# Attention value products with stationary values, heads in pairs on the two halves of the output rows

## The reference, cut to what matters

```
logits = einsum('bqhd,bqkhd->bhqk', q, k_sel) * scale - slopes * dist
p = softmax(logits, axis=-1)
return einsum('bhqk,bqkhd->bqhd', p, v_sel)      # per head: probabilities times values
...
o = concatenate([o_a, o_b], axis=-1)
return o @ w_out
```

## Time and profile before

| | |
|---|---|
| median of 3 runs | 2524.43 us (2522.5 to 2528.1) |
| the profiled execution: its own time | 2525.57 us |
| its span (first to last instruction) | 2523.8 us, 35771 instructions |
| PE busy | 2448.3 us, 97% of the span, 13860 matmul records |
| DVE, ACT, POOL busy | 1185.3 us (47%), 951.8 us (38%), 1053.6 us (42%) |
| `mixers` on PE | from about 468 to 940 us of the span |
| products with values, L1314 | 576 records, between 503.3 and 907.9 us |

### The profile page before, as it was taken

One profiled execution on the slowest core, in us unless ns is written; L12 is line 12 of the kernel. 1 busy time (PEld: TensorE's weight loads), 2 busy tenths in 40 slices (PEclk: granted clock), 3 DMA queues, 4 the chain that ended last, 5 costly groups with the idle time before them and its releaser, 6 DMA issues.

```text
span 2523.8 us, 35771 instructions
## 1 busy us (share of the span) xinstructions
PE 2448.3 (97%) x13860; PEld 2107.5 (84%) x13860; DVE 1185.3 (47%) x2304; ACT 951.8 (38%) x1614; POOL 1053.6 (42%) x584
## 2 busy tenths in 40 slices
PE   7999999889999989999999999999999999999996
PEld 7889999768888778899998888888888888888885
DVE  6798985445555433333333365323365432232224
ACT  3687883333443323322223333322333222332222
POOL 0434123365554314443343544444444444355342
PEclk9999999899999999999999999999999999999999
DMA  4101230334333233323332323232333233333431
GB/s 140 35 18 38 99 100 29 104 97 129 105 102 104 81 108 113 113 84 89 96 101 84 92 75 117 84 109 82 93 101 101 75 109 100 100 93 107 117 93 50
DMA packets 275000, 231.40 MB, mean 92 GB/s; under 512 B 10768, under 2 KB 255568, under 8 KB 274832
## 3 DMA queue, kind: packets, MB, share of 16 engines
q1 hardware_dynamic: 266640, 220.59, 29.3%
q10 hardware_dynamic: 8192, 8.52, 1.0%
HBM read 215.81 MB, written 12.71 MB: 91 GB/s over the span
## 4 chain that ended last, share of the span: by engine, by line
PE 60%; DMA 1%; ACT 1%; POOL 1%; DVE 1%; issue 0%; POOLq 0%; SPq 0%; ACTq 0%; DVEq 0%
PE banks L2043 38%; PE banks L2077 19%; PE banks L2109 1%; PE banks L1764 1%; DMA last_draw<-in_w_down 0%; PE banks L2068 0%; PE banks L2071 0%; POOL dL L1986 0%; PE banks L2095 0%; DMA cq_raw<-in_w_up 0%; POOL wL L1979 0%; ACT dH L2161 0%; DVE y L2301 0%; ACT hH L1774 0%; DVE n_bn L1673 0%
## 5 line engine op out<-in xcount | busy, mean ns | idle before, releaser
L1979 POOL TENSOR_TENSOR wL<-cq_raw,wH 128x2048 fp32r<-128x2048 f32 x87 | 407.8, 4687 | 521.5 <-ACT wH L2155 521.5
L2043 PE MATMUL banks<-hL,wH 128*128 128x512 f32 (+1 forms) x1760 | 619.2, 352 | 5.9 <-ACT hid L2170 3.2
L2043 PE MATMUL banks<-hH,wL 128*128 128x512 f32 (+1 forms) x1760 | 618.0, 351 | 0.0
L2043 PE MATMUL banks<-hH,wH 128*128 128x512 f32 (+1 forms) x1760 | 616.2, 350 | 0.0
L2043 PEld LDWEIGHTS banks<-hL,wH 128*128 128x128 f32 x1760 | 331.4, 188 | 55.2 <-ACT hid L2170 4.1
L2275 DVE TENSOR_TENSOR hid<-hid,banks 128x512 f32<-128x512 f32 (+1 forms) x110 | 64.3, 584 | 657.7 <-PE banks L2043 552.0
L2043 PEld LDWEIGHTS banks<-hH,wL 128*128 128x128 f32 x1760 | 331.2, 188 | 46.3
L2043 PEld LDWEIGHTS banks<-hH,wH 128*128 128x128 f32 x1760 | 331.8, 189 | 44.9
L1986 POOL TENSOR_TENSOR dL<-last_draw,dH 128x1024 fp32r<-128x1024 f32 x88 | 221.0, 2511 | 318.2 <-ACT dH L2161 318.1
L2301 DVE TENSOR_TENSOR y<-y,banks 128x512 f32<-128x512 f32 (+1 forms) x340 | 232.1, 686 | 181.5 <-PE banks L2077 180.3
L2161 ACT ACTIVATE dH<-last_draw 128x1024 fp32r<-128x1024 f32 x88 | 93.3, 1061 | 504.0 <-PE banks L2077 326.1
(11 more groups left out here) (277 smaller groups left out, 4151.6 us busy)
## 6 DMA issues: line engine op xcount, KB each, us to landing
cq_raw<-in_w_gate SPq DMA_DIRECT2D x88, 512.0 KB, 4.4
cq_raw<-in_w_up SPq DMA_DIRECT2D x88, 512.0 KB, 5.9
last_draw<-in_w_down SPq DMA_DIRECT2D x88, 512.0 KB, 3.4
w_out_part<-in_w_out SPq DMA_DIRECT2D x60, 512.0 KB, 4.0
va<-in_w_in SPq DMA_DIRECT2D x10, 1024.0 KB, 5.4
va<-in_x SPq DMA_DIRECT2D x8, 512.0 KB, 4.4
vg_scratch<-y ACTq DMA_DIRECT2D x32, 128.0 KB, 1.7
y<-in_x SPq DMA_DIRECT2D x8, 512.0 KB, 8.2
```

The costliest lines, as they stand in the source:

```text
L1979: nc.gpsimd.tensor_tensor(wL[:, ff % 2, :, :, :].rearrange("p g k f -> p (g k f)"), raw[:, :, :, :].rearrange("p g k f -> p (g k f)"), wH[ ...
L2043: last = nc.tensor.matmul(banks[:, GU + (2 * q + g) % 3, 0:n], wt[:, ff % 2, g, k, :], h[:, k, a:a + n], start=(k == 0 and part == 0), sto ...
```

## The change

The operands of the value products change places. Values become the stationary operand, 64 columns of one head; turned probabilities, 128 columns, move. The result is features as rows, tokens as columns. Two heads that stand next to each other write to rows 0 to 63 and 64 to 127 of the same 128 columns of bank PV. `pv(i)` of every step becomes `pv_pair(i)` of every odd step, which takes both heads, their matmuls in turn. `pv_meta` becomes four matmuls of 128 columns. pT gets a third slot.

Since the result is no longer in token rows, the inverse sums, one per token and head, cannot be a multiplier per row. `normed` now copies bank PV straight to oT. The job `ot_att` no longer transposes: eight matmuls, each with one column of inverse sums repeated 64 times as stationary operand and the identity as moving one, spread the inverses over 64 rows each. A new function of DVE, `shared_out`, multiplies oT by them in place. It stands in DVE's stream of the step behind `turned`; ACT's copy is gone. o_tok is gone.

```
@@ mixers
+    TS = 3
-    pT = sb(c, "pT", [P, 2, NT, P])
+    pT = sb(c, "pT", [P, TS, NT, P])
-    o_tok = sb(c, "o_tok", [P, 2, A_WIDTH])
+    def pairs_to(i):
+        return max(i - A_HEADS + 2, 0) // 2
@@ SP
-                sp.wait_ge(pv_done, turned_to(NU - 1))
+                sp.wait_ge(pv_done, pairs_to(NU - 1))
@@ PE, on_shared
             if what == "ot_att":
-                pe.wait_ge(otok_done, m + 1)
+                pe.wait_ge(rs_done, m + 1)
                 for f in range(4):
-                    last = nc.tensor.transpose(banks[:, SHARED, f * P:f * P + n], o_tok[0:n, s, f * P:(f + 1) * P],
-                                               ident[0:n, 0:n])
+                    for par in range(2):
+                        share = rsums[0:n, s, 2 * f + par:2 * f + par + 1].to_broadcast([n, HD])
+                        last = nc.tensor.matmul(banks[HD * par:HD * (par + 1), SHARED, f * P:f * P + n], share, ident[0:n, 0:n],
+                                                start=True, stop=True)
@@ PE
-        def pv(i):
+        def pv_pair(i):
             m, h = units[i]
+            f = h // 2
             pe.wait_ge(t_act, turned_to(i))
             if dve_turns(i):
                 pe.wait_ge(t_dve, dve_turns(i))
-            if h == 0:
+            if f == 0:
                 pe.wait_ge(otok_done, m)
             for j in range(1, m + 1):
-                last = nc.tensor.matmul(banks[:, PV, h * HD:(h + 1) * HD], pT[:, i % 2, j, :],
-                                        va[:, j, h * HD:(h + 1) * HD], start=(h == 0 and j == 1), stop=False)
+                for par in range(2):
+                    last = nc.tensor.matmul(banks[HD * par:HD * (par + 1), PV, f * P:(f + 1) * P],
+                                            va[:, j, (2 * f + par) * HD:(2 * f + par + 1) * HD], pT[:, (i - 1 + par) % TS, j, :],
+                                            start=(f == 0 and j == 1), stop=False)
             last.then_inc(pv_done, 1)
@@ PE, pv_meta
-            nc.tensor.matmul(banks[0:n, PV, :], meta_pT[:, 0:n], meta_v[:, :], start=(m == 0), stop=True).then_inc(meta_done, 1)
+            for f in range(4):
+                last = nc.tensor.matmul(banks[:, PV, f * P:f * P + n], meta_v[:, f * P:(f + 1) * P], meta_pT[:, 0:n],
+                                        start=(m == 0 and f == 0), stop=(f == 3))
+            last.then_inc(meta_done, 1)
@@ PE, loop over the steps
-            if A_HEADS + 2 <= i <= NU + 1:
-                pv(i - 2)
+            if A_HEADS + 2 <= i <= NU + 1 and (i - 2) % 2:
+                pv_pair(i - 2)
@@ ACT, turned, and the same wait in DVE's turned
-            if turned_to(i - 2):
-                act.wait_ge(pv_done, turned_to(i - 2))
+            if pairs_to(i - TS):
+                act.wait_ge(pv_done, pairs_to(i - TS + 1))
@@ ACT, off_shared and loop
-            if what == "ot_att":
-                if m >= 2:
-                    act.wait_ge(shared_psum, nth["op", m - 2, 3])
-                ins_ = nc.scalar.activation(oT[:, m % 2, 0:4, 0:n], four(src)[:, :, 0:n], ACT.Copy)
-            early = shared_job(m, h) if h in (3, 5) else None
+            early = shared_job(m, h) if h == 3 else None
@@ DVE, normed
+                dve.wait_ge(shared_psum, nth["op", m - 2, 3])
+            nc.vector.reciprocal(rsums[0:n, m % 2, :], sums[0:n, m % 2, :]).then_inc(rs_done, 1)
+            dve.wait_ge(meta_done, m + 1)
+            nc.vector.tensor_copy(oT[:, m % 2, 0:4, 0:n], four(banks[:, PV, :])[:, :, 0:n]).then_inc(otok_done, 1)
@@ DVE
+        def shared_out(m):
+            n = TILES[m][1]
+            dve.wait_ge(shared_psum, nth["ot_att", m])
+            dve.wait_ge(otok_done, m + 1)
+            at = oT[:, m % 2, 0:4, 0:n]
+            nc.vector.tensor_tensor(at, at, four(banks[:, SHARED, :])[:, :, 0:n], ALU.mult).then_inc(shared_done, 1)
@@ DVE, loop over the steps
             if 1 <= i <= NU:
                 turned(i - 1)
+            if shared_job(m, h) and shared_job(m, h)[0] == "ot_att":
+                shared_out(m - 1)
             if out_job(m, h):
                 out_added(*out_job(m, h))
```

More of the change, by code:

```diff
@@ L1386, in turned @@
             act.wait_ge(t_psum, turned_to(i))
-            if turned_to(i - 2):
-                act.wait_ge(pv_done, turned_to(i - 2))
+            if pairs_to(i - TS):
+                act.wait_ge(pv_done, pairs_to(i - TS + 1))
             k = min(PER_BANK, m)
-            nc.scalar.activation(pT[:, i % 2, 1:1 + k, :], banks[:, T_LO, 0:k * P].rearrange("p (f t) -> p f t", f=k), ACT.Copy)\
+            nc.scalar.activation(pT[:, i % TS, 1:1 + k, :], banks[:, T_LO, 0:k * P].rearrange("p (f t) -> p f t", f=k), ACT.Copy)\
               .then_inc(t_act, 1)
@@ L1469, in _ @@
                 gates(m + 1, h)
-            if shared_job(m, h) and h and not early:
+            if shared_job(m, h) and h and not early and shared_job(m, h)[0] != "ot_att":
                 off_shared(*shared_job(m, h))
@@ L1528, in turned @@
                 dve.wait_ge(t_psum, turned_to(i))
-                if turned_to(i - 2):
-                    dve.wait_ge(pv_done, turned_to(i - 2))
+                if pairs_to(i - TS):
+                    dve.wait_ge(pv_done, pairs_to(i - TS + 1))
                 k = m - PER_BANK
-                nc.vector.tensor_copy(pT[:, i % 2, 1 + PER_BANK:1 + m, :],
+                nc.vector.tensor_copy(pT[:, i % TS, 1 + PER_BANK:1 + m, :],
                                       banks[:, T_HI, 0:k * P].rearrange("p (f t) -> p f t", f=k)).then_inc(t_dve, 1)
@@ L1537, in normed @@
             dve.wait_ge(exp_done, A_HEADS * (m + 1))
-            nc.vector.reciprocal(rsums[0:n, m % 2, :], sums[0:n, m % 2, :]).then_inc(rs_done, 1)
-            dve.wait_ge(rs_done, m + 1)
-            dve.wait_ge(meta_done, m + 1)
             if m >= 2:
                 dve.wait_ge(shared_psum, nth["ot_att", m - 2])
[L1543 to L1546, removed]
+                dve.wait_ge(shared_psum, nth["op", m - 2, 3])
[8 more added lines that the diff above has]
+            nc.vector.tensor_tensor(at, at, four(banks[:, SHARED, :])[:, :, 0:n], ALU.mult).then_inc(shared_done, 1)
         def gates(m, stage):
```

## The result

The changed kernel takes 2535.23 us (median of 20 runs, 2527.39 to 2539.36), the kernel before 2525.02 us (20 runs, 2522.5 to 2530.2). The ratio is 1.0032, interval 1.0024 to 1.0039: slower by 0.3%, a little more than the bound of 0.2%. (The medians alone give 1.0040, since the median of the changed kernel lies in the slower of the two groups told of next.) The profiled execution took 2538.29 us; its span is 2536.5, 12.7 over that of before.

What follows compares the result with a forecast made beforehand. PE's stream was taken to bound the kernel. Terms -14.7 + 7.7 + 12.9 + 0.9 = +6.8 us on the profiled 2525.57 gave 2532.4; the median of runs lying 1.1 lower, the forecast was 2531.3 us, range 2518 to 2549.

Steps and rivals of the forecast that it cites:

- One burst for two heads: Value products: a pair's two column halves run at once, costing one head's burst, 0.22 to 1.78 us by tile.
- Change-over of 0.35: Pairs at h = 1, 3, 7: going in and out of half-column bursts costs 0.35 us each, 22 times, +7.7 us.
- Even steps: h = 0, 2, 6 lose their burst, limited by the next late link: 6.3, 3.0 and 5.4 us, together -14.7.
- Step 5: h = 5, tiles 2 to 8: the op behind the pair waits for DVE's product; +12.9 us in sum.
- The tail: End of the mixer stage: eight matmuls and a DVE product replace a copy of ACT, +0.9 us.
- the free change-over: Rival at the 22 pairs: column halves need no change-over, -7.7 and -0.3 us, 2523.3 us; chance 0.15.
- The halves in turn: Rival at the pairs: column halves run one after the other, a second burst each, +33.5 us, 2564.8 us; chance 0.15.
- The open weight loads: Rival at the pairs: weight loads of the halves are not covered, 280 x 0.054 = +15 us, 2546.4 us; chance 0.08.
- A product of DVE that isn't late: Rival at h = 5: DVE's backlog shrinks, the step gives about 0 instead of +12.9, 2518.4 us; chance 0.07.
- 0.41 + 0.23: Chances that the changed kernel is slower, summed in the prediction to 0.62, less 0.02 for underread gains: 0.60.

Runs made afterwards that it cites:

- split pairs: Changed kernel with the jobs of h = 4 and 5 exchanged, each pair of tiles 2 to 8 cut into two bursts around the turn: 2528.45 us.
- the exact wait: Changed kernel, but each copy into pT waits only for the pair that last read its slot, not one unit more: 2531.94 us.
- the reordered kernel: Changed kernel, but a pair does all key tiles of one head, then all of the other, instead of alternating: 2552.54 us.
- the four with exchanged jobs: Jobs of h = 4 and 5 swapped: in the changed kernel 2522.37 us, plus narrower pT waits 2520.81, plus pairs in two bursts 2528.45; in the kernel before 2529.96.

## Why the prediction was right, and where it was off

The forecast was 2531.3 us, in a range of 2518 to 2549, and slower at 0.6. The median is 2535.23, slower. The range and the direction held, but 2531.3 lies in the empty space between the two groups of runs: the median of the faster group alone is 3.6 us over the kernel before (2528.6), that of all runs 10.2, and the forecast was 6.3. By the steps:

- **One burst for two heads: right.** The earlier trace rows was the fit row. The pairs take 1.89 us in tile 9. The estimate of 1.26 bursts from the Trainium skill (TensorE: Matmul & The Clock Gate, Part 3, measured speedup) for two tiles would be 2.2 us for the same pair; the 1.89 measured are 1.09 bursts of the 1.73 in the earlier trace rows, part of the change-over in it. (The mean of 0.1115 us a record, and with it 1.78 for this burst, was read too high: from its first record to the next work a burst takes 0.39 us for 4 records and 1.73 for 16, some 0.05 less than the formula each.)
- **Change-over of 0.35: nearly right.** The split pairs give 0.30, and steps of h = 1 and 7 where nothing else is late +0.29 to +0.36. 22 x 0.30 is 6.6, not 7.7.
- **Even steps: h = 0 and 6 right in sum, h = 2 under-read.** h = 0 is -5.9 over tiles 2 to 8 (the 6.3 had 5.5 for them and 0.8 for tile 9), and h = 6 is -5.5 for -5.4. Step 2 came out at -6.7, not -3.0, and step 3 at +4.7 where the change-overs alone make 2.45. The burst goes from one step and part of the wait for it stands in the step behind, so only the two together can be compared: -2.0 for -0.55, a gain of 1.5 us that I had not. I had priced the two steps apart. "In tiles 2 to 4 nothing is gained" held for the two together (-0.01, +0.04 and +0.15), but I had charged them +0.35 each with nothing against it. Against it stand waits that shrank: those for ACT in step 3 from 0.25, 0.33 and 0.15 to 0.05, 0.16 and none over 0.04, and in tile 3 one of 0.29 for DVE's o_tok in step 2, which went. No run takes these apart.
- **Step 5: right in the wait and in size, in tile 5 not in what the product stands behind.** Predicted with step 4 +12.9, in tiles 2 to 8 +2.9, +2.7, +1.75, +1.35, +0.9, +0.8, +2.5; measured, with the clock's share out of tiles 3 and 8, +2.6, +2.5, +1.5, +1.2, +1.0, +0.9, +2.5, sum 12.2. The edits that shorten the wait or take it away give the time back, each as far as it does so. In tile 5 I had DVE's pT copy waiting for the pair. It does not wait there (the copy begins at 708.74, right behind the copy into S, and the exact wait changes the step by 0.01 us): DVE's backlog makes the product late, and that the +1.35 came near the +1.2 is luck. In tiles 6 to 8 the copy waits as I said, 0.28 us in tile 6 and more behind.
- **The tail: right but for the clock.** From step 7 of tile 8 on I had +0.8 (0.9 for the eight matmuls and the product, 2 x 0.35, less 0.8 at the start of tile 9); it is 4.2 longer, 2.9 of it clock, which leaves 1.3. In front of the product DVE has two products of the recurrence's norm that wait for ACT until 926.44, which I had not looked at; they fit the half microsecond more. "Copies that nobody waited for" was wrong here as well: in the tail of the kernel before PE waits 1.50 us for that copy of ACT.
- **The clock: missing.** The sum took every term at 2.4 GHz. Three of the waits that the change makes or lengthens were followed by stretches at 1.2 GHz, 6.3 us in the profiled execution. The terms at full clock give +6.4 on the span where I had +6.8, and the rest of the profiled execution's +12.7 is this. That 6.4 and 6.8 are so near is partly luck: 1.2 of the 6.4 lie ahead of the changed steps and in the trunk, where nothing was forecast, and they hide most of the 1.5 missed in steps 2 and 3. The median of the runs came out at +10.2 because the runs differ in the clock, as the two groups at 0.991 and at 0.987 say. That the three stretches are what parts the groups is not shown: no run of the faster group has a trace here, the medians of the groups lie 9.2 us apart and not 6.3, and the stretches, 13.6 us at half clock, lower the mean clock by 0.003 where the groups differ by 0.005.

The rivals: the free change-over fell with the split pairs. The halves in turn fell by the 32 records of 1.89 us; the reordered kernel shows what that case looks like. The open weight loads fell with them: records on one half begin 0.11 us apart while both halves run, so the loads of the column halves are covered. The Trainium skill (TensorE: Matmul & The Clock Gate, Part 3, what overlaps) has loads overlap only where row groups differ; here they don't differ, and the measurement decides. A product of DVE that isn't late was not this kernel but nearly became true by moving it: 2526.54 with the product early, 2522.37 with the job a step earlier. I had 2518.4 for it, and the kernel without the product had 2518.38; that they agree so closely is chance, for steps 4 and 5 still cost 3.5 us there where the rival had about none.

Two sums of the prediction don't come out. The second bursts of h = 5 in tiles 5 to 8, in the price of the halves in turn, make 5.8 us and not 9, so that rival stood for 2561.6 and not 2564.8 us. And in the chances 0.41 + 0.23 is 0.64, not 0.62.

## What to carry to other kernels

Ask of a value that gates a shared bank or an op not how long its instruction is, but what stands ahead of it in its engine's stream: here an instruction of 0.69 us, put behind a backlog, cost 17 us with what came behind its waits (2535.23 with it, 2518.38 without), more than the 7.7 us that the 32 us less of products bring without it, and one job moved to the step where nothing waits for it turned a loss of 0.3% into a gain of 0.2%. Matmuls on two column halves run at once if they alternate, and each burst of them costs 0.30 us in and out, so make few, long bursts. Where PE's stream gets long waits that it didn't have (here 1.6 to 2.6 us), put the price of a slower clock behind them into the range, and look at the single runs for a second group. Compare a step that loses work together with the step behind it, where the wait may stand.

## What the runs showed of the hardware that I had not expected

- Halves whose matmuls come one head after the other still overlap by four records of either head at the seam: 0.35 to 0.37 us for bursts of 0.62 to 1.73 us.
- Behind a wait of the same length the clock fell in one execution and not in another. The timeline of the kernel with the exact wait has, in tile 3 and in the tail:

```profile
602.34 3.72 PE L1245 MATMUL banks<-w_out_part,oT 128*128 128x256 f32 x16 [1.59 <-DVE oT L1558]
...
919.78 5.11 PE L1245 MATMUL banks<-kaT,oT 128*128 128x256 f32 x16 [2.63 <-DVE oT L1558]
```

  The first wait is the 1.60 us of the kernel after, where the op behind it took 5.41; here it took 3.72. In the tail part of the op ran at the lower clock in both. The traces together: the wait of 2.21 us in tile 8 was followed by a fall in all five kernels that have it; the one of 2.6 us in the tail had a fall with it in three of four; of five waits of 1.6 to 1.8 us in tiles 2 and 3, one. Between tile 3 and the end of the stage the kernel before and the four with exchanged jobs have no wait of PE over 1.5 us and no fall. But the kernel with the heads in turn has a fall in tile 8 with no wait of PE over 0.9 us in the 20 us ahead of it, and none in the tail behind 2.63 us. Its step 1 of tile 8 is 4.4 us longer than in the kernel after, of which the second burst explains some 1.2 (windows view, then the timeline):

```profile
855.00:862.00 7.00, 7.00 (x38) 6.67 (x38) 0.00 (x0) 0.60 (x1) 0.00 (x0) 0.51 0.00 0
...
852.22 0.40 PE L1252 MATMUL banks<-kaT,qaT 128*128 128x16 f32 x2 [0.41 <-DVE nmax L1517]
...
858.75 4.41 PE L1322 MATMUL banks<-pT,va 128*64 128x128 f32 x28
...
945.36 3.72 PE L1245 MATMUL banks<-kaT,oT 128*128 128x256 f32 x16 [2.63 <-DVE oT L1558]
```

  So in these traces a long wait goes with a fall more often than not, but is neither needed for one nor enough. What decides it stays open.
- The eight matmuls with 64 stationary columns take 1.03 us for 16 records from start to start (881.91 to 882.94), 0.064 each with the change-over in it, so two of them run at once as well.
